# Pooling mixers of a four-layer trunk: bands of 240 to 272 columns in place of bands of 100, and the input's squares summed by rows

## The reference

```python
def trailing_mean(xg, win):
    L = xg.shape[1]
    cs0 = jnp.pad(jnp.cumsum(xg.astype(jnp.float32), axis=1), ((0, 0), (1, 0), (0, 0)))
    lagged = jnp.pad(cs0, ((0, 0), (win, 0), (0, 0)))[:, 1:L + 1]
    count = jnp.minimum(jnp.arange(1, L + 1), win).astype(jnp.float32)[None, :, None]
    return (cs0[:, 1:] - lagged) / count

def pool_mixer(h, w, b, scale):              # windows 2, 4, 8, 16, one for each group of 256 channels
    for g, win in enumerate(POOL_WINDOWS):
        hg = h[..., g * POOL_GROUP:(g + 1) * POOL_GROUP]
        groups.append(trailing_mean(hg, win).astype(h.dtype) - hg)
    pooled = jnp.stack(groups, axis=2)
    mixed = jnp.einsum('blgc,gcd->blgd', pooled, w).reshape(B_, L, D_MODEL)
    return (mixed + b) * scale
...
    for i in range(DEPTH):
        y = rmsnorm(h, norm_mix_g[i])
        ...                                  # y = the layer's mixer of y
        h = h + y
        h = h + swiglu_ffn(rmsnorm(h, norm_ffn_g[i]), ffn_w_gate[i], ffn_w_up[i], ffn_w_down[i])
    return rmsnorm(h[:, N_META:], final_norm_g)
```

## Time and profile before

| | us |
|---|---|
| median of 3 runs (2152.8 to 2157.08) | 2156.8 |
| the profiled execution, device time | 2154.58 |
| its span from first to last instruction | 2152.9 |
| layer 0: start to the first L820 | 30.5 |
| layer 0: L820, five tiles | 30.5 to 46.6 |
| layer 0: the windows | 46.6 to 70.0 |
| layer 0: the first products of the feed-forward part, with the sums | 70.0 to 85.3 |
| layer 3: the windows | 1759.6 to 1784.2 |
| layer 3: the first products | 1784.2 to 1797.6 |

### The profile page before, as it was taken

How to read it: one execution, slowest core, us unless ns; L and a number is a source line. 1 busy time by engine, 2 the same in 40 slices (tenths; PEclk the granted TensorE clock), 3 DMA queues, 4 the chain that set the end, 5 groups by cost and what they waited for, 6 DMA issues and landing times.

```text
span 2152.9 us, 40602 instructions
## 1 busy us (share of the span) xinstructions
PE 2087.3 (97%) x15970; PEld 2019.1 (94%) x15970; DVE 1622.0 (75%) x2295; ACT 849.2 (39%) x1268; POOL 244.4 (11%) x361
## 2 busy tenths in 40 slices
PE   7999999999998899999999999999999989999997
PEld 6999999998886899999999999999999988899996
DVE  5687778767776479777969896588887866977794
ACT  5243343334444234333445443343433343433341
POOL 3100000322122410000050000200000140000003
PEclk8799999999998899999999998999999988999999
DMA  3333342332121133333341120224423222333332
GB/s 106 110 89 92 113 117 79 89 109 60 49 59 49 40 92 86 98 97 97 94 123 40 39 59 20 79 79 119 117 75 101 84 70 63 98 98 97 98 96 91
DMA packets 306395, 181.51 MB, mean 84 GB/s; under 512 B 6556, under 2 KB 303517, under 8 KB 306278
## 3 DMA queue, kind: packets, MB, share of 16 engines
q1 hardware_dynamic: 304702, 175.01, 28.3%
q10 hardware_dynamic: 1048, 2.71, 0.3%
q0 software_dynamic: 528, 2.16, 0.3%
HBM read 177.74 MB, written 4.81 MB: 85 GB/s over the span
## 4 chain that ended last, share of the span: by engine, by line
PE 76%; DVE 9%; DVEq 6%; issue 5%; ACT 2%; DMA 1%; POOLq 0%; POOL 0%; SPq 0%; ACTq 0%
PE ps L767 40%; PE ps L1015 28%; DVEq L2344 3%; PE ps L850 2%; DVE cv L2345 1%; PE ps L820 1%; PE ps L1174 1%; DVEq L2007 1%; PE ps L789 1%; PE ps L1150 1%; DVE w_lo L1971 1%; DMA w_raw<-in_ffn_w_down 1%; DVEq L1976 1%; DVE y_lo L1971 1%; DVE scores L2122 0%
## 5 line engine op out<-in xcount | busy, mean ns | idle before, releaser
L1015 PE MATMUL ps<-t_lo,y_hi 128*128 128x264 f32 (+1 forms) x1008 | 285.7, 283 | 0.0
L1015 PE MATMUL ps<-t_lo,w_hi 128*128 128x264 f32 (+1 forms) x1008 | 285.7, 283 | 0.0
L1015 PE MATMUL ps<-t_hi,w_lo 128*128 128x264 f32 (+1 forms) x1008 | 285.4, 283 | 0.0
L1015 PE MATMUL ps<-t_hi,y_lo 128*128 128x264 f32 (+1 forms) x1008 | 285.3, 283 | 0.0
L1015 PE MATMUL ps<-t_hi,w_hi 128*128 128x264 f32 (+1 forms) x1008 | 285.1, 283 | 0.1
L767 PE MATMUL ps<-hid_hi,w_hi 128*128 128x264 f32 (+1 forms) x1232 | 284.3, 300 | 0.5 <-DVE hid_lo L2027 0.4
L1015 PE MATMUL ps<-t_hi,y_hi 128*128 128x264 f32 (+1 forms) x1008 | 284.8, 283 | 0.0
L767 PE MATMUL ps<-hid_lo,w_hi 128*128 128x264 f32 (+1 forms) x1232 | 283.6, 300 | 0.0
L767 PE MATMUL ps<-hid_hi,w_lo 128*128 128x264 f32 (+1 forms) x1232 | 283.1, 299 | 0.0
L1529 ACT ACTIVATE w_hi<-w_raw 128x1024 fp32r<-128x1024 f32 (+1 forms) x108 | 127.8, 1201 | 329.6 <-PE ps L767 193.5
L767 PE MATMUL ps<-y_hi,w_hi 128*128 128x264 f32 (+1 forms) x1088 | 244.2, 301 | 9.9 <-DVE cv L2317 3.8
(11 more groups left out here) (282 smaller groups left out, 4499.2 us busy)
## 6 DMA issues: line engine op xcount, KB each, us to landing
w_raw<-in_ffn_w_gate SPq DMA_DIRECT2D x88, 512.0 KB, 5.0
w_raw<-in_ffn_w_up SPq DMA_DIRECT2D x88, 512.0 KB, 4.7
w_raw<-in_ffn_w_down SPq DMA_DIRECT2D x64, 512.0 KB, 4.3
w_raw<-in_ffn_w_down SPq DMA_DIRECT2D x32, 384.0 KB, 4.0
...
```

The source lines that it names most:

```text
L1015: mm = pe.matmul(ps[:, bank, 0:hw], w[:, at:at + P], b[:, t, k, 0:hw], start=k == 0 and n == 0, stop=k == 3 and n == 2)
```

## The change

**Tiles.** The five tiles of tokens start at 0, 128, 241, 369 and 497, with 128, 128, 128, 128 and 31 rows. They serve the input rows, too: `x_rows` holds the five tiles (meta rows ahead in the first), so that SP issues six DMAs for them, the last of them of 31 rows, and PE's turned tiles stand in PSUM as one run of 528 columns over two banks.

**Bands.** `bands` holds for each window two bands with zeros around them, at such places that any tile's matmul takes 256 or 272 columns of it. `windows(d)` puts columns 0 to 255 in one bank (tiles 0 and 1, and 16 columns for the rest of the first tile's edge) and the 272 others in the next (tiles 2, 3 and 4), and adds up what all tiles give. A block is 11 matmuls, ten of them of 256 or 272 columns. Two pairs of banks take turns (4 and 5, 6 and 7), and block d from 2 on waits until DVE has read block d-2.

**Memory.** `bands` is 12.5 KB of each partition and lies where other layers put their own things. ACT writes it to DRAM in layer 0, and POOL reads it back in layer 2's last stage, behind a wait for its first tile, with a DMA of its own queue.

**Sums of the input's squares.** ACT squares the five tiles of input rows and adds each row up in the same instruction (`accum_out`) into `tok_x`. PE's 20 products with ones, DVE's four additions and the reduction go. Tile 3 of layer 0 no longer waits for `rstd_ready`.

**Order.** All windows are now called from `head_by_blocks`, still ahead of its first product. DVE's splits of the next layer's two first weight tiles stand ahead of blocks 0 and 1.

The core of the diff:

```diff
+OVER = CUT - EDGE + 1
 TILES = 5
-STEP = (TOK - P) // (TILES - 1)
...
+TILE_STARTS = (0, P, OVER, OVER + P, OVER + 2 * P)
+TILE_ROWS = (P, P, P, P, TOK - OVER - 2 * P)
...
-            for i in range(QT):
-                sp.dma_start(m.x_rows[:, i, :], a["x"][0, i * P:(i + 1) * P, :]).then_inc(s.x_in, 16)
-            sp.dma_start(m.meta_rows[:, :], a["meta_tokens"]).then_inc(s.x_in, 16)
+            sp.dma_start(m.x_rows[0:META, 0, :], a["meta_tokens"]).then_inc(s.x_in, 16)
+            sp.dma_start(m.x_rows[META:P, 0, :], a["x"][0, 0:P - META, :]).then_inc(s.x_in, 16)
+            for i in range(1, TILES):
+                t, n = TILE_STARTS[i] - META, TILE_ROWS[i]
+                sp.dma_start(m.x_rows[0:n, i, :], a["x"][0, t:t + n, :]).then_inc(s.x_in, 16)
...
+            pool.wait_ge(s.bands_out, 16)
+            pool.wait_ge(s.tile_used, first["down2"] + 1)
+            pool.dma_start(m.bands[:, :, :], bands_dram).then_inc(s.bands_in, 16)
             sum_squares(R_POOL3, H_FFN2)
...
+            def windows(d, which, hn):
+
+                g, base = d // 2, 4 + 2 * (d % 2)
+                low, high = ps[:, base, CUT:512], ps[:, base + 1, 0:WIDE]
...
+                if d >= 2:
+                    pe.wait_ge(s.h_ready, NB * hn + d - 1)
+                hi, lo = z_of(0)
+                pe.matmul(low, hi, m.bands[:, g, FIRST0:FIRST0 + CUT], start=True, stop=False)
+                pe.matmul(low, lo, m.bands[:, g, FIRST0:FIRST0 + CUT], start=False, stop=False)
+                pe.matmul(low[:, 0:EDGE], hi, m.bands[:, g, LOW0:BANDS], start=False, stop=False)
+                for i, out, c0, c1 in ((1, low, 0, CUT), (2, high, 0, WIDE), (3, high, 0, WIDE), (4, high, 0, WIDE)):
+                    hi, lo = z_of(i)
+                    at = BAND0 + c0 + (CUT if i > 1 else 0) - TILE_STARTS[i]
+                    for n, z in enumerate((hi, lo)):
+                        mm = pe.matmul(out[:, c0:c1], z, m.bands[0:TILE_ROWS[i], g, at:at + c1 - c0],
+                                       start=i == 2 and n == 0, stop=i in (1, 4) and n == 1)
+                mm.then_inc(s.pooled, 1)
...
-                    act.activation(m.band[:, :, :], m.band_raw[:, :, :], ACT.Copy)
-                    act.activation(m.edge_hi[:, :, :], m.edge_raw[:, :, :], ACT.Copy).then_inc(s.band_hi_ready, 1)
+                    act.activation(m.bands[:, :, 0:LOW0], m.bands_raw[:, :, :], ACT.Copy).then_inc(s.band_hi_ready, 1)
...
-            squares(s.h_ready, 0, m.h, m.x_square)
+            act.wait_ge(s.tok_cleared, 1)
+            act.wait_ge(s.x_in, 16 * (TILES + 1))
+            for i, n in enumerate(TILE_ROWS):
+                e = act.activation(m.row_squares[0:n, i, :], m.x_rows[0:n, i, :], ACT.Square,
+                                   accum_out=m.tok_x[0:n, i:i + 1])
+            e.then_inc(s.token_sums, 1)
...
                 for d in range(NB):
+                    if d < 2:
+                        split_lo(tile0 + 4 + d, 0, 0, cols[tile0 + 4 + d])
                     add_windows(d)
-                    if d in (1, 3):
-                        c = 4 + d // 2
-                        split_lo(tile0 + c, 0, 0, cols[tile0 + c])
                     if d > 0:
                         y_lo(d - 1, yn, row, 0, TOK)
```

More of the change, by code:

```diff
@@ L199, in __init__ @@
         new = Placer(nc, keep, end)
-        self.x_rows = new("x_rows", [P, QT, D])
-        self.meta_rows = new("meta_rows", [META, D])
-        self.vec_rows = new("vec_rows", [ROWS, D])
+        self.z_hi = new("z_hi", [P, TILES, D], F32R)
+        z_lo_at = new.offset
+        self.z_lo = new("z_lo", [P, TILES, D], F32R)
+        self.bands = new("bands", [P, 4, BANDS], F32R)
+        self.x_square = new("x_square", [P, NB * TOK])
         self.lam_rows = new("lam_rows", [P, 4, HEAD_DIM])
@@ L406, in pool_sums @@
 def pool_sums(r):
-    return sum(x not in SUMS_OF_PAIRS for x in range(r))
+    return sum(x not in SUMS_OF_PAIRS + SUMS_OF_ROWS for x in range(r))
 def squares_before(r):
@@ L777, in sum_tokens, with sum_squares @@
                 for n, t in enumerate(starts):
-                    mm = pe.matmul(ps[:, bank, n:n + 1], m.sumsq[:, t:t + P], m.ones[:, 0:1], start=True, stop=True)
+                    if t + P > TOK:
+                        pe.matmul(ps[:, bank, n:n + 1], m.sumsq[:, TOK - P:TOK], m.ones[:, 0:1], start=True, stop=True)
+                    rows = min(P, TOK - t)
+                    mm = pe.matmul(ps[0:rows, bank, n:n + 1], m.sumsq[:, t:t + rows], m.ones[:, 0:1], start=True,
+                                   stop=True)
                 mm.then_inc(s.token_sums, 1)
-            def sum_squares(r, square, between=None, starts=(0, 128, 256, 384, TOK - P)):
+            def sum_squares(r, square, between=None):
                 nth = SUMS_OF_PAIRS.index(r)
@@ L807, in rows_times_weights @@
                     base = 2 * (i % 4)
-                    if i == 3:
+                    rows = TILE_ROWS[i]
+                    if i == 3 and r not in SUMS_OF_ROWS:
                         pe.wait_ge(s.rstd_ready, r + 1)
@@ L878, in convolve, with pair_layer @@
                 mm.then_inc(s.conv_done, 1)
-            def pair_layer(name, n, e0, r, yn, hn, t0, half, conv=False):
+            def pair_layer(name, n, e0, r, yn, hn, t0, half, conv=False, pooled=None):
                 tile0 = first[name]
                 def head_by_blocks():
-                    pe.wait_ge(s.h_ready, NB * hn + 4)
+                    if pooled is None:
+                        pe.wait_ge(s.h_ready, NB * hn + 4)
+                    else:
+                        for d in range(NB):
+                            windows(d, pooled, hn)
                     pe.wait_ge(s.lo_ready, tile0 + 2)
```

172 lines of the change are left out of this document (81 added, 91 removed).

## The result

| | before | changed |
|---|---|---|
| median of the runs | 2157.1 us (9 runs, 2152.8 to 2160.2) | 2146.8 us (9 runs, 2137.6 to 2158.0) |
| the profiled execution | 2154.6 | 2150.2 |

What follows compares the result with a forecast made beforehand. PE, with narrow pooling windows at the low clock, was taken as the bound: 2154.6 - 1.7 - 7.3 - 2.5 - 9.3 - 2.3 = 2131.5 us, so a median of 2133, range 2124 to 2146.

Steps and rivals of the forecast that it cites:

- Which clock: Pooling layers' new wide windows: PE's granted clock taken as 1.00, though PE is busy for only two thirds.
- rival C: Both layers' windows: clock falls in PE's gaps, a block takes 2.35 us; 2145, in one layer only 2139; chance 0.17.
- the -7.3 and -2.5 of layer 0: Layer 0: windows 7.3 us shorter at 2.0 us a block, first products behind them 2.5 us shorter at full clock.
- The start: Up to the end of block 0's windows, layer 0: 8.70 us of products removed, input later at 15.0; net -1.7 us.
- DVE and POOL: Windows: POOL's 1.30 us holds DVE's `y_lo` of 0.69, so 2.0 us a block; layer 3's windows 9.3 us shorter.
- first products: Layer 3, behind the windows: matmuls at full clock instead of 4.90 us at 0.50, so 2.3 us shorter.
- The costs put at nothing: `bands` stored in layer 0 and read back before layer 3, 1.6 MB each, and the issues of ACT and POOL: 0 us.
- The gate's rule: PE's clock goes by recent busyness and gaps lose it; set aside because narrow matmuls at 100% busy read 0.50.

Runs made afterwards that it cites:

- e2_before_fill: The kernel before plus 18 unused matmuls of 256 columns per pooling layer, ahead of the last tile of z: 2155.1 us, ratio 0.999 to 1.001.
- e1_fill: The changed kernel plus 18 unused matmuls of 264 columns per pooling layer, in the gap ahead of the last tile's windows: 2137.9 us.
- e5_split31: The changed kernel with the input's last 31 rows moved by two DMAs, of 16 and 15 rows, instead of one: 2140.8 us.
- e6_pool_short: e4_rows128 with POOL adding only 8 of 528 columns of squares behind the two pooling layers, so norms are wrong: 2126.6 us.
- e4_rows128: The changed kernel with a last tile of 128 tokens instead of 31, the 97 repeated tokens masked to 0: 2131.7 us.

## Why the prediction was wrong

**The bound now, and what the clock does.** Right in its reading, wrong in the step "Which clock. ... I take 1.00". The windows' clock came out at 1.00 in layer 3 and at 0.50 in layer 0, which is rival C in one of the layers, for which I had 2139, and 0.17 for C as a whole. The evidence that I took was of the wrong kind. That 6.80 us with PE busy for 3.86 read 1.00 shows that such a stretch *can* keep the clock, not that it always will; and the gap ahead of the last tile's windows, 1.11 us in the earlier trace rows, is at the place where the clock fell in layer 0. In layer 3 of the kernel before, where it fell as well, that gap is only 0.33 us:

```profile
1761.55 0.31 PE L850 MATMUL ps<-band,z_hi 128*128 128x100 f32 x1 [0.33 <-DVE z_lo L1866]
```

I put the fall down to narrow matmuls alone. e2_before_fill shows that they do lose it, a few us later; by e1_fill the gap is what lost it in the changed kernel, though not in every run. By the mean clock of its runs, the -7.3 and -2.5 of layer 0 didn't come in six of the nine runs.

**The size of a block at the low clock.** Rival C had 2.35 us; it is 3.02, by the changes of rows. With 2.35 even a low clock would have given 3.4 to 3.9 us in layer 0; it gave 0.3. So C in one layer was put at 2139, and the median is 2146.8.

**The start.** The DMA of 31 rows was right (15.0 against 14.65, and 10.57 without it). What failed is the stage of the turned rows, for which the sum keeps the time of before: 10.3 us from the landing to the end of DVE's last operation on them, less 2.6 for the additions, plus 0.5, is 8.2. It took 11.0 (14.65 to 25.65). 1.8 us of that is the change of rows, the rest a pace of PE that didn't rise as it had before. Less the 0.35 by which the input landed sooner, that is the 2.5 by which this term is off. The Trainium skill's rule on how many engines a transfer uses ("DMA: Bandwidth & Descriptors", section "Why a DMA increments its semaphore by 16 and not by 1") agrees with e5_split31: 31 rows are late, 16 and 15 are not.

**DVE and POOL.** Right: 2.0 us a block and 13.3 us of windows in layer 3 (13.1), and first products 2.1 shorter (2.3). The hold is shown by e6_pool_short.

**The costs put at nothing.** `bands` was in time and cost nothing. What was missed is outside the change: the clock's falls in layers 1 and 2, worth 3.4 us more in this execution than in that of the kernel before. The forecast put that stretch at 0 without a reason.

**The gate's rule.** The Trainium skill, "TensorE: Matmul & The Clock Gate", Part 1, has gaps as what loses the clock. I set it aside because narrow matmuls at 100% busy ran at 0.50. Both hold here: e1_fill shows the gap, e2_before_fill the narrow matmuls. One row that contradicts a rule as the only cause did not make the other cause go away.

With the clock kept in both layers the changed kernel is at 2138 (e1_fill), and without the 31 rows at 2131 to 2132 (e4_rows128), near the 2133 of the forecast. That is not the forecast come true: there block 0's windows end 4.7 us earlier than before, not 1.7.
